# A decoder layer on one core: the first two weight blocks loaded in slices on a second DMA queue, TensorE's first units behind finer waits, and the first norm's squares added by VectorE

## The reference

```python
def rmsnorm(x, g):
    y = xf * lax.rsqrt(jnp.mean(xf * xf, axis=-1, keepdims=True) + EPS)
    return (y * g.astype(jnp.float32)).astype(x.dtype)
...
xn = rmsnorm(x, mix_norm_g[l])
p = xn @ w_in[l]
```

## Time and profile before

| what | value |
|---|---|
| median of 3 timed runs | 1036.73 us (1036.67 to 1036.95) |
| the profiled execution's own time | 1038.42 us |
| its span in the trace | 1036.7 us |
| TensorE matmuls busy | 1019.0 us, 98% |
| VectorE, ScalarE, GpSimd busy | 57%, 41%, 7% |
| chain that ended last, share of TensorE | 93% |

### The profile page before, as it was taken

How to read it: one execution, slowest core, us unless ns; L and a number is a source line. 1 busy time by engine, 2 the same in 40 slices (tenths; PEclk the granted TensorE clock), 3 DMA queues, 4 the chain that set the end, 5 groups by cost and what they waited for, 6 DMA issues and landing times.

```text
span 1036.7 us, 12635 instructions
## 1 busy us (share of the span) xinstructions
PE 1019.0 (98%) x4724; PEld 837.8 (81%) x4724; DVE 593.2 (57%) x764; ACT 424.3 (41%) x515; POOL 67.6 (7%) x74
## 2 busy tenths in 40 slices
PE   8999999999999999999999999989999999999996
PEld 7897888887777887777888888868888888888886
DVE  6835754656676566556364456687656666543323
ACT  5514445644435322444432333544444344332331
POOL 5610000000000000000000000320000000000002
PEclk9999999999999999999999999989999999999998
DMA  6332222223222333343252222513233222253312
GB/s 238 114 113 70 82 84 82 77 93 105 89 85 82 120 122 124 132 132 103 81 183 87 97 88 97 181 61 119 85 100 101 100 86 88 68 176 94 102 56 81
DMA packets 32024, 108.24 MB, mean 104 GB/s; under 512 B 3684, under 2 KB 5860, under 8 KB 31600
## 3 DMA queue, kind: packets, MB, share of 16 engines
q1 hardware_dynamic: 29520, 93.86, 27.1%
q0 software_dynamic: 2320, 13.69, 4.0%
q10 hardware_dynamic: 144, 0.14, 0.1%
HBM read 103.42 MB, written 4.25 MB: 104 GB/s over the span
## 4 chain that ended last, share of the span: by engine, by line
PE 93%; DVE 4%; ACT 2%; issue 1%; DMA 1%; DVEq 0%; SPq 0%; ACTq 0%
PE gb L413 81%; PE gb L446 4%; DVE w_lo L985 1%; PE xb L596 1%; PE gb L524 1%; PE xb L556 1%; PE xb L549 1%; PE xb L536 1%; PE xb L413 1%; ACT w_hi L701 1%; PE xb L513 1%; DMA raw<-w_stream 1%; DVE y_lo L993 1%; PE gb L464 1%; PE xb L584 0%
## 5 line engine op out<-in xcount | busy, mean ns | idle before, releaser
L985 DVE TENSOR_TENSOR w_lo<-raw,w_hi 128x1024 fp32r<-128x1024 f32 (+2 forms) x181 | 218.1, 1206 | 342.8 <-ACT w_hi L701 342.4
L701 ACT ACTIVATE w_hi<-raw 128x1024 fp32r<-128x1024 f32 (+2 forms) x181 | 183.8, 1017 | 413.5 <-PE gb L413 380.8
L413 PE MATMUL gb<-xn_hi,w_hi 128*128 128x512 f32 x720 | 285.0, 396 | 0.0
L413 PE MATMUL gb<-xn_hi,w_lo 128*128 128x512 f32 x720 | 281.1, 390 | 0.0
L413 PE MATMUL gb<-xn_lo,w_hi 128*128 128x512 f32 x720 | 281.0, 390 | 0.0
L413 PE MATMUL gb<-y_hi,w_hi 128*128 128x512 f32 x400 | 159.1, 398 | 6.0 <-DVE y_lo L993 4.2
L413 PEld LDWEIGHTS gb<-xn_hi,w_hi 128*128 128x128 f32 x720 | 135.8, 189 | 29.7 <-issue 1.0
L413 PEld LDWEIGHTS gb<-xn_lo,w_hi 128*128 128x128 f32 x720 | 135.8, 189 | 29.0 <-issue 1.4
L413 PEld LDWEIGHTS gb<-xn_hi,w_lo 128*128 128x128 f32 x720 | 135.6, 188 | 28.6
L413 PE MATMUL gb<-y_lo,w_hi 128*128 128x512 f32 x400 | 156.6, 391 | 0.0
L413 PE MATMUL gb<-y_hi,w_lo 128*128 128x512 f32 x400 | 156.4, 391 | 0.0
(11 more groups left out here) (231 smaller groups left out, 1018.4 us busy)
## 6 DMA issues: line engine op xcount, KB each, us to landing
raw<-w_stream SPq DMA_DIRECT2D x149, 512.0 KB, 3.3
raw<-w_down SPq DMA_DIRECT2D x16, 384.0 KB, 3.0
abc<-scr_a POOLq DMA_DIRECT2D x8, 640.0 KB, 4.1
raw<-w_down SPq DMA_DIRECT2D x16, 320.0 KB, 2.8
x_in<-xT SPq DMA_DIRECT2D x8, 256.0 KB, 6.5
x<-xT POOLq DMA_DIRECT2D x1, 2048.0 KB, 8.5
scr_x<-x POOLq DMA_DIRECT2D x1, 2048.0 KB, 7.4
x<-scr_x POOLq DMA_DIRECT2D x1, 2048.0 KB, 8.4
```

What stands on the lines that cost most here:

```text
L413: ins = pe.matmul(out, w[:, r, lo:hi], rhs(k)[x], start=(first and n == 0 and q == 0), stop=(last_ and n == len(ks) - 1 and q == 2))
L701: act.activation(w_hi[:, r, 0:n], raw[:, r, 0:n], ACT.Copy).then_inc(S["hi_ready"], 1)
L985: dve.tensor_tensor(w_lo[:, r, 0:n], raw[:, r, 0:n], w_hi[:, r, 0:n].bitcast(F32), ALU.subtract)\
```

## The change

It has five parts. (1) Units 0 and 1 are no longer loaded by SP. ScalarE issues them, each in three slices of 128, 256 and 640 columns (blocks k = 0, k = 1 and 2, k = 3 to 7), in the order head0_0, head1_0, head0_1, head1_1, head0_2, head1_2, behind a `vec` cut to its first 28 columns; SP loads the other 236 behind units 2 and 3 (`vec_rest`). SP thus issues x blocks 0 to 7 in a row. (2) ScalarE and VectorE make `w_hi` and `w_lo` slice by slice, between the blocks of x. (3) TensorE waits per slice and per operand. (4) ScalarE writes the squares to a buffer of their own, `sq1`, for all 8 blocks, and VectorE adds them in four additions; GpSimd's additions are gone. (5) The sum over partitions moves from behind unit 2 into the middle of unit 3. GpSimd's `rsm` load goes behind its memsets.

```diff
@@ -43,6 +43,8 @@
 NEG = -1e30
 
 LINE = 512
+SLICE = [(0, 128), (128, 384), (384, 1024)]
+SLICE_OF = [0, 1, 1, 2, 2, 2, 2, 2]
 A_HEADS, C_HEADS, D_HEADS = 4, 8, 4
 A_SCALE = 64 ** -0.5
 D_SCALE = 128 ** -0.5
@@ -196,6 +198,7 @@
+    sq1 = at("sq1", [P, KD, T], F32, base + 3 * RING * 4096)
@@ -293,8 +296,9 @@
     def _(sp):
         for k in range(KD):
             sp.dma_start(x_in[:, k, :], xT[:, k, :]).then_inc(S[f"x{k}"], 16)
-            for r in {0: (0, 1), KD - 1: (2, 3)}.get(k, ()):
-                sp.dma_start(raw[:, r, :], w_stream[r]).then_inc(S[f"raw{r}"], 16)
+        for r in (2, 3):
+            sp.dma_start(raw[:, r, :], w_stream[r]).then_inc(S[f"raw{r}"], 16)
+        sp.dma_start(vec[:, V_BCW:], vecs[:, V_BCW:]).then_inc(S["vec_rest"], 16)
 
         with sp.Fori(1, U_DOWN // RING) as i:
             for r in range(RING):
@@ -320,20 +324,10 @@
 
     @block.gpsimd
     def _(pool):
-        pool.dma_start(rsm[:], rowsm).then_inc(S["rsm_loaded"], 16)
         pool.memset(ones[:], 1.0).then_inc(S["built"], 1)
         pool.memset(cst[:, 0:1], 1.0).then_inc(S["built"], 1)
         pool.memset(cst[:, 1:2], EPS).then_inc(S["built"], 1)
-
-        for k in range(KD):
-            pool.wait_ge(S["n1_sqr"], k + 1)
-            sq = (nmb, enb)[k % 2]
-            if k == 0:
-                ins = pool.tensor_copy(stg[:, 0, :], sq[:])
-            else:
-                ins = pool.tensor_tensor(stg[:, 0, :], stg[:, 0, :], sq[:], ALU.add)
-            ins.then_inc(S["n1_acc"], 1)
-            pool.wait_ge(S["n1_acc"], k + 1)
+        pool.dma_start(rsm[:], rowsm).then_inc(S["rsm_loaded"], 16)
 
         pool.wait_ge(S["n1_rstd"], 1)
         for k in range(KD):
@@ -472,12 +466,22 @@
         for _ in range(12):
             pe.matmul(X[3][:, 0:P], ones[:], ones[:], start=True, stop=True)
 
+        def head(u, k, w, x, first, last_):
+
+            return pe.matmul(GB[u][:, :], w[:, u, k * P:k * P + P], xg(k)[x], start=first, stop=last_)
+
         for k in range(KD):
+            n = SLICE_OF[k]
+            pe.wait_ge(S["xg_hi"], k + 1)
+            for u in (0, 1):
+                pe.wait_ge(*((S["hi_ready"], u + 1) if n == 2 else (S["head_hi"], 2 * n + u + 1)))
+                head(u, k, w_hi, 0, k == 0, False)
+            for u in (0, 1):
+                pe.wait_ge(*((S["lo_ready"], u + 1) if n == 2 else (S["head_lo"], 2 * n + u + 1)))
+                head(u, k, w_lo, 0, False, False)
             pe.wait_ge(S["xg_ready"], k + 1)
             for u in (0, 1):
-                if k == 0:
-                    pe.wait_ge(S["lo_ready"], u + 1)
-                ins = gemm(GB[u][:, :], u, k * P, xg, [k], first=(k == 0), last_=(k == KD - 1))
+                ins = head(u, k, w_hi, 1, False, k == KD - 1)
         ins.then_inc(S["unit_done"], 2)
 
         for u in range(U_OUT):
@@ -487,13 +491,16 @@
                     pe.wait_ge(S[need], cnt)
             if u == U_DV:
                 pe.wait_ge(S["xn_ready"], KD)
-            if u >= 2:
+            if u >= 2 and u != 3:
                 unit(u)
-            if u == 2:
-
-                pe.wait_ge(S["n1_acc"], KD)
+            if u == 3:
+
+                pe.wait_ge(S["lo_ready"], u + 1)
+                gemm(GB[u][:, :], u, 0, xg, range(4), last_=False)
+                pe.wait_ge(S["n1_acc"], 1)
                 pe.wait_ge(S["built"], 3)
                 pe.matmul(X[0][:, :], ones[:], stg[:, 0, :], start=True, stop=True).then_inc(S["n1_sum"], 1)
+                gemm(GB[u][:, :], u, 4 * P, xg, range(4, KD), first=False).then_inc(S["unit_done"], 1)
 
             if u == 22:
                 pe.wait_ge(S["g_rows"], 1)
@@ -697,7 +704,7 @@
 
         def hi(u, r, rep, n=1024):
 
-            act.wait_ge(S[f"raw{r}"], 16 * rep + 16)
+            act.wait_ge(S[f"raw{r}"], 16 * rep + (0 if r < 2 else 16))
             act.activation(w_hi[:, r, 0:n], raw[:, r, 0:n], ACT.Copy).then_inc(S["hi_ready"], 1)
 
         def rstd(out, summed, n):
@@ -707,27 +714,41 @@
             return act.activation(out, out, ACT.Exp, scale=-0.5)
 
 
-        act.dma_start(vec[:], vecs).then_inc(S["vec_loaded"], 16)
+        act.dma_start(vec[:, 0:V_BCW], vecs[:, 0:V_BCW]).then_inc(S["vec_loaded"], 16)
+        for n, (lo_, hi_) in enumerate(SLICE):
+            for u in (0, 1):
+                act.dma_start(raw[:, u, lo_:hi_], w_stream[u][:, lo_:hi_]).then_inc(S[f"head{u}_{n}"], 16)
         table(EXP_LN)
+
+        def head(u, n):
+
+            c = slice(*SLICE[n])
+            act.wait_ge(S[f"head{u}_{n}"], 16)
+            act.activation(w_hi[:, u, c], raw[:, u, c], ACT.Copy)\
+                .then_inc(S["hi_ready" if n == 2 else "head_hi"], 1)
+
+        def square(k):
+
+            act.activation(sq1[:, k, :], x_in[:, k, :], ACT.Square).then_inc(S["n1_sqr"], 1)
+
+        head(0, 0)
         act.wait_ge(S["vec_loaded"], 16)
-
-        def square(k):
-            if k >= 2:
-                act.wait_ge(S["n1_acc"], k - 1)
-            act.activation((nmb, enb)[k % 2][:], x_in[:, k, :], ACT.Square).then_inc(S["n1_sqr"], 1)
         for k in range(KD):
             act.wait_ge(S[f"x{k}"], 16)
             act.activation(y_hi[k // 4][:, k % 4, :], x_in[:, k, :], ACT.Identity, scale=gain(V_MIX, k))\
                 .then_inc(S["xg_hi"], 1)
             if k == 0:
-                hi(0, 0, 0)
-                hi(1, 1, 0)
-            if k < 4:
-                square(k)
-        for r in (2, 3):
-            hi(r, r, 0)
-            square(2 * r)
-            square(2 * r + 1)
+                head(1, 0)
+            elif k < 3:
+                head(0, k)
+                head(1, k)
+            else:
+                square(k - 3)
+        hi(2, 2, 0)
+        square(5)
+        square(6)
+        hi(3, 3, 0)
+        square(7)
         act.wait_ge(S["built"], 3)
         act.wait_ge(S["n1_sum"], 1)
         rstd(stg[:, 1, :], X[0][:, :], D).then_inc(S["n1_rstd"], 1)
@@ -749,6 +770,7 @@
             elif U_XBC <= u < U_XBC + 8:
                 c = u - U_XBC
                 if c == 0:
+                    act.wait_ge(S["vec_rest"], 16)
                     act.wait_ge(S["a_out"], 16)
                     act.wait_ge(S["psum_read_dve"], order[first_tile[U_DV]][1])
                 if c >= 2:
@@ -994,16 +1016,32 @@
                                             op0=ALU.mult, op1=ALU.subtract)
 
 
+        def head(u, n):
+
+            c = slice(*SLICE[n])
+            dve.wait_ge(*((S["hi_ready"], u + 1) if n == 2 else (S["head_hi"], 2 * n + u + 1)))
+            dve.tensor_tensor(w_lo[:, u, c], raw[:, u, c], w_hi[:, u, c].bitcast(F32), ALU.subtract)\
+                .then_inc(S["lo_ready" if n == 2 else "head_lo"], 1)
+
+        head(0, 0)
+        head(1, 0)
         dve.wait_ge(S["vec_loaded"], 16)
         for k in range(KD):
             dve.wait_ge(S["xg_hi"], k + 1)
             split_gain(y_lo[k // 4][:, k % 4, :], x_in[:, k, :], V_MIX, k, y_hi[k // 4][:, k % 4, :])\
                 .then_inc(S["xg_ready"], 1)
-            if k == 0:
-                lo(0, 0)
-                lo(1, 1)
-        for r in (2, 3):
-            lo(r, r)
+            if 1 <= k < 3:
+                head(0, k)
+                head(1, k)
+        lo(2, 2)
+        dve.wait_ge(S["n1_sqr"], 4)
+        link(dve.tensor_tensor(sq1[:, 0:2, :], sq1[:, 0:2, :], sq1[:, 2:4, :], ALU.add))
+        dve.wait_ge(S["n1_sqr"], 6)
+        link(dve.tensor_tensor(sq1[:, 0:2, :], sq1[:, 0:2, :], sq1[:, 4:6, :], ALU.add))
+        lo(3, 3)
+        dve.wait_ge(S["n1_sqr"], KD)
+        link(dve.tensor_tensor(sq1[:, 0:2, :], sq1[:, 0:2, :], sq1[:, 6:8, :], ALU.add))
+        dve.tensor_tensor(stg[:, 0, :], sq1[:, 0, :], sq1[:, 1, :], ALU.add).then_inc(S["n1_acc"], 1)
 
         def evac(u):
 
@@ -1049,6 +1087,8 @@
             elif U_XBC <= u < U_XBC + 8:
 
                 c = u - U_XBC
+                if c == 0:
+                    dve.wait_ge(S["vec_rest"], 16)
                 w = stg[:, c % 2, :]
                 dve.wait_ge(S["x_tap"], c + 1)
                 for back in (1, 2, 3):
```

More of the change, by code:

```diff
@@ L246, in build @@
     scr_a = nc.dram_tensor("scr_a", [8, PACK], F32).ap()
-    names = """raw0 raw1 raw2 raw3 x0 x1 x2 x3 x4 x5 x6 x7 vec_loaded rsm_loaded built filled masks masks_r
+    names = """raw0 raw1 raw2 raw3 x0 x1 x2 x3 x4 x5 x6 x7 head0_0 head1_0 head0_1 head1_1 head0_2 head1_2 head_hi head_lo vec_loaded vec_rest rsm_loaded built filled masks masks_r
         hi_ready lo_ready unit_done psum_read_dve psum_read_act act_own dve_own
```

## The result

The changed kernel takes 1040.33 us (median of 8 runs, 1038.71 to 1041.66) against 1037.31 of the kernel before in the same sessions (8 runs, 1036.67 to 1038.29). The ratio is 1.0025, 95% interval 1.0015 to 1.0036: slower by 1.5 to 3.7 us. The profiled execution has 1040.64 us and a span of 1038.8. The kernel before had 1036.73 in its first three runs, so 0.6 us of the distance to the forecast is in the kernel before too, and is not the change's. One execution of a later run, one_queue, took 2087.74 us, twice the others; its ratio leaves that one out, and nothing on record explains it.

What follows compares the result with a forecast made beforehand. TensorE, holding 93% of the chain, was taken as the bound, so unit 4's start decides: the start gains 1.9 us, the new hole takes 2.0, giving 1036.8, set at 1036.6 us; range 1034.2 to 1038.6.

Steps and rivals of the forecast that it cites:

- (f): Ahead of unit 4: moving the sum half a unit opens a new TensorE hole of 2.0 us.
- rival C: Behind the new hole ahead of unit 4: the clock falls, costing 1.7 us more, 1038.5; chance 0.22.
- forecast A: Whole kernel: start gain 1.9 us against hole 2.0, last slice at 10.6 to 12.6, 1035.8 to 1037.8; chance 0.40.
- D: As a rival, loading phase: second queue gets less than row for row, slice at 12.8 or later, 1038.0 to 1039; chance 0.13.
- D = 11.6: Loading phase: the moment, in us, at which the last slice, head1_2, was expected to land.
- Term (b): Loading phase: queues share row for row, 2.90 MB through at 10.6 us, last slice at 11.6; bounds 9.65 and 12.8.
- 1.0 us of lateness: Loading phase: a slice is seen 1.0 us after the byte count has it through, taken from unit 1 before.
- the forecast 34.07: Start of unit 4 in us, as D + 22.47 with D = 11.6, against 33.97 before.
- Lateness for small slices: Loading phase: small slices more likely land sooner than 1.0 us late, so the time was set 0.2 us lower.
- the share goes by rows: Loading phase: two queues share row for row, so SP moves seven x blocks beside ScalarE's seven transfers.
- The upper bound: Loading phase: SP getting four rows for three, 3.4 MB, lands the last slice at 12.8 us.
- ScalarE's five pairs at 1.14: Ahead of unit 2: five y_hi and square pairs, 5.70 us, make ScalarE set unit 2, not TensorE, by 0.5 us.

Runs made afterwards that it cites:

- one_queue: The changed kernel with the six slices issued by SP, each pair behind x blocks 0, 1 and 2, moved sum kept: 1037.95 us, ratio 1.0006 to the kernel before.
- sum_back: The changed kernel with the norm's sum put back behind unit 2: 1036.99 us, ratio 0.9998 to the kernel before.
- sum_moved_alone: The kernel before with one edit, the sum moved from behind unit 2 into the middle of unit 3: 1041.39 us, ratio 1.0035 to the kernel before.
- hole_filled: The changed kernel with 4 matmuls of ones, never read, ahead of unit 4: 1038.74 us, ratio 1.0013 to the kernel before.

## Why the prediction was wrong

**The step that failed is the clock's term in the sum behind (f), which was put at nothing.** The hole itself was forecast: 2.0 us, released by `dq`; it measured 1.89. Its second price, the clock, stood as rival C with 0.22, and the forecast A was made without it. The changed kernel's profile shows 1.7 us of it. And C and D were priced one at a time: C at D = 11.6, 1038.5, which set the end of the range. Both came (D was 12.77), and by the prediction's own terms that is 1039.7. Its threshold was stated: C decides for slower from D = 11.9 on.

What the runs showed in its place: unit 4 starts 1.5 us later and 1.7 us are lost to the clock, 3.2 together, against 3.0 between the medians. sum_back and sum_moved_alone show that this hangs on the moved sum, and the clock falls behind unit 4 in none of the eight profiles that have no hole there. That the hole lowers the clock each time is not so: it did in the changed kernel and in sum_moved_alone and did not in one_queue. The price of the early holes, which C took from the earlier trace rows, is not fixed either; sum_moved_alone has the holes without it. What decides between a hole that is followed by a low clock and one that isn't stays open. The Trainium skill (TensorE: Matmul & The Clock Gate, Part 1) has the throttled state as the default and activity as what releases it; the falls behind idle time agree with that (0.57 behind the hole here), and the 1.00 in one_queue behind an equal one shows that the length of a hole alone does not tell.

**Term (b) was mis-sized.** The last slice landed at 12.77, not 11.6. The windows have moved 0.262 x 2.4 + 0.308 x 4.3 + 0.405 x 2 = 2.76 MB by 10.7 us, against 2.95 before: from 4.4 to 8.7 us the engines were busy for 0.93 of the time instead of 1.01, and moved 308 / 0.93 = 331 GB/s while busy instead of 374. With the same 1.0 us of lateness 3.2 MB lay ahead of the last slice instead of 2.9. That puts unit 4 1.2 us later, and with 0.2 in the steps behind it the forecast 34.07 becomes 35.45. A part of this is chance: with the same loads the last slice's copy started at 11.9 us in hole_filled and 12.8 here. Lateness for small slices I had argued down by 0.2; in all five such profiles the last slice came later than 11.6. That the share goes by rows held. The upper bound was summed wrong: seven transfers at four rows for three are 2.45 MB of x, and with 1.06 that makes 3.5, not 3.4, so it should have been 13.1 us and not 12.8. The Trainium skill (DMA: Bandwidth & Descriptors, "Issuing engines are not separate DMA queues") has a second issuer save only issue time. The runs agree in that the second queue moved nothing more, 2.76 MB by 10.7 us against 2.95; what it changed is which rows came first.

**What held.** ScalarE's five pairs at 1.14 and not TensorE set unit 2: D + 8.7. The issues cost nothing by themselves: ScalarE was free at 5.49, long ahead of its last slice. VectorE's additions ended at 26.9, ahead of the sum's turn at 29.8, and cost nothing; my remark that they would be just late behind unit 2 was a hair off, sum_back shows them just in time. vec_rest landed near 16 us and cost nothing. There is no clock of 0.50 ahead of 20 us. That did less for the start than the windows suggest, 0.3 us as sum_moved_alone shows. The warm-up began 1.3 us earlier and not 0.7; TensorE did not set unit 2, so nothing hung on it.

**The sum, corrected.** Start +0.7, hole -1.9 and 0.3 of overlap lost behind unit 2 (together -1.5), clock -1.7, late stretch +1.2 in this pair of profiles: 2.0, measured 2.1 in span. The clusters at 1038.8 and 1040.3 and above in the changed kernel's runs are read as executions without and with the fall; only one of them was looked at in a profile, so that is argued and not shown.

## What to carry to other kernels

Before moving a reduction's last step later, add up the whole chain that hangs on it, to the next reader of its bank, and compare it with the work left beside it: here 5.6 us of chain lost 2.7 of its cover of 6.3. A wait of TensorE of some 2 us can cost nearly that again in clock, as it did in two of three profiles here; matmuls nobody reads, in half of the gap, took 1.2 to 2.1 us off the time, but not in each execution. So judge such a fill by many runs and not by one profile. When two queues load side by side, count the rows ahead of the transfer that matters, not only the bytes, and split off no more pieces than are needed: six slices landed between 11.9 and 12.8 us, four at 10.7. And before a low stretch of the clock is booked as a loss, look at what TensorE would have waited for without it.

## What the runs showed that I had not expected

The warm-up's matmuls took 5.10 / 24 = 0.21 us for each record, though the windows there show a clock of 1.00; the same matmuls later took 1.05 / 8 = 0.13. The clock's own record in that trace begins only near 7 us, so the 1.00 ahead of it is not a measurement; that the warm-up ran at the lower level until then fits its pace, but is not shown. Four fillers sized by the warm-up thus covered 1.0 us, not 1.7, and nine covered 2.2, not 3.8. And the late hole's stretch at the lower clock differs from one execution to the next, 1.7 us of loss in the changed kernel's profile and 2.9 in that of before, with the same program around it.
